# Where the high activations of the projections begin in SBUF: 64 instead of 192 modulo 256 bytes

## The reference

```python
# block 1
proj = rms_norm(x, norm1_w) @ w_in          # 2048 -> 5648 columns
attn = moba_attention(q, k, v)              # 8 heads of 128; one block of 256, so causal attention
y    = ssd_chunked_scan(xs, dt, a, bm, cm)  # 16 heads of 64, state 128
x = x + concatenate([attn, ssm]) @ w_out    # 2048 -> 2048
u = causal_dwconv(rms_norm(x, norm2_w) @ w_up, ...)       # 2048 -> 11264
x = x + (silu(u_gate) * u_val) @ w_down     # 5632 -> 2048
# block 2
mod = silu(c) @ w_ada + b_ada               # shift, scale, gate
proj = (rms_norm_2(x, g) * (1 + scale) + shift) @ w_in    # 2048 -> 7168 columns
y_a, y_r = dilated attention (8 heads), retention in both directions (4 heads)
out = rms_norm_2(x + gate * (concatenate([y_a * silu(z_a), y_r * silu(z_r)]) @ w_out), final_gain)
```

## Time and profile before

| | us |
|---|---|
| median of three runs | 1658.18 |
| the profiled execution, device time | 1657.61 |
| its span, first to last instruction | 1655.9 |
| TensorE busy with matmuls | 1608.4 |
| VectorE busy | 1159.8 |
| ScalarE busy | 807.2 |

### The profile page before, as it was taken

How to read it: one execution, slowest core, us unless ns; L and a number is a source line. 1 busy time by engine, 2 the same in 40 slices (tenths; PEclk the granted TensorE clock), 3 DMA queues, 4 the chain that set the end, 5 groups by cost and what they waited for, 6 DMA issues and landing times.

```text
span 1655.9 us, 33704 instructions
## 1 busy us (share of the span) xinstructions
PE 1608.4 (97%) x13254; PEld 1578.9 (95%) x13254; DVE 1159.8 (70%) x1357; ACT 807.2 (49%) x973; POOL 26.3 (2%) x53
## 2 busy tenths in 40 slices
PE   7999999989999999999999999999799999999997
PEld 7998899989999999999999999999799999999996
DVE  6676677765678888888888888676664544664755
ACT  6444355544554544545445454444454543445542
POOL 0000000000000000000000000000000000000000
PEclk9999999999999999999999999999999999999998
DMA  8453344455548777787777775555455555355451
GB/s 344 138 177 128 128 151 143 153 181 187 182 164 334 261 267 293 254 303 267 261 284 260 304 267 206 189 189 181 150 181 189 185 185 170 136 165 173 159 179 51
DMA packets 85187, 336.17 MB, mean 203 GB/s; under 512 B 9456, under 2 KB 9712, under 8 KB 78704
## 3 DMA queue, kind: packets, MB, share of 16 engines
q1 hardware_dynamic: 77328, 281.05, 49.0%
q0 software_dynamic: 7056, 51.38, 8.4%
q10 hardware_dynamic: 720, 2.52, 0.4%
HBM read 332.82 MB, written 2.10 MB: 202 GB/s over the span
## 4 chain that ended last, share of the span: by engine, by line
PE 72%; DVE 5%; issue 2%; ACT 1%; DVEq 0%; ACTq 0%
PE PS L1096 23%; PE PS L1098 23%; PE PS L1100 23%; DVE ada_w L931 1%; DVE wlo L586 1%; ACT whi L254 1%; PE PS L1197 1%; DVE UV L889 1%; PE PS L1164 1%; PE PS L1342 0%; DVE X L1083 0%; PE PS L1183 0%; DVE X L602 0%; DVE rb L620 0%; PE PS L1143 0%
## 5 line engine op out<-in xcount | busy, mean ns | idle before, releaser
L1096 PE MATMUL PS<-gh,whi 128*128 128x256 f32 x3520 | 999.4, 284 | 14.5 <-DVE wlo L586 9.4
L1098 PE MATMUL PS<-gl,whi 128*128 128x256 f32 x3520 | 985.1, 280 | 0.0
L1100 PE MATMUL PS<-gh,wlo 128*128 128x256 f32 x3520 | 983.9, 280 | 0.0
L586 DVE TENSOR_TENSOR wlo<-raw,whi 128x1024 fp32r<-128x1024 f32 x528 | 644.8, 1224 | 432.0 <-ACT whi L254 430.6
L254 ACT ACTIVATE whi<-raw 128x1024 fp32r<-128x1024 f32 x528 | 557.4, 1059 | 731.0 <-PE PS L1100 728.4
L1096 PEld LDWEIGHTS PS<-gh,whi 128*128 128x128 f32 x3520 | 664.5, 189 | 21.8 <-issue 20.5
L1098 PEld LDWEIGHTS PS<-gl,whi 128*128 128x128 f32 x3520 | 663.5, 188 | 2.8 <-issue 1.9
L1100 PEld LDWEIGHTS PS<-gh,wlo 128*128 128x128 f32 x3520 | 663.0, 188 | 0.0
L1096 PE MATMUL PS<-ah,whi 128*128 128x256 f32 x704 | 197.5, 281 | 10.5 <-DVE UV L889 6.8
L1098 PE MATMUL PS<-al,whi 128*128 128x256 f32 x704 | 196.1, 279 | 0.0
L1100 PE MATMUL PS<-ah,wlo 128*128 128x256 f32 x704 | 196.0, 278 | 0.0
(11 more groups left out here) (187 smaller groups left out, 804.3 us busy)
## 6 DMA issues: line engine op xcount, KB each, us to landing
raw<-weights SPq DMA_DIRECT2D x528, 512.0 KB, 3.4
ada_w<-w_ada POOLq DMA_DIRECT2D x48, 1024.0 KB, 5.1
outT<-X SPq DMA_DIRECT2D x4, 512.0 KB, 2.6
X<-xT SPq DMA_DIRECT2D x3, 512.0 KB, 8.8
c<-const ACTq DMA_DIRECT2D x1, 1536.0 KB, 6.7
c_act<-c_rows POOLq DMA_DIRECT2D x1, 1024.0 KB, 9.0
X<-xT SPq DMA_DIRECT2D x2, 256.0 KB, 4.9
prm<-params ACTq DMA_DIRECT2D x1, 276.5 KB, 4.2
```

The source lines that it names most:

```text
L586: dve.tensor_tensor(wlo[:, j % SPLIT, :], raw[:, j, :], whi[:, j % SPLIT, :].bitcast(F32), ALU.subtract).then_inc(s_lo, 1)
L1096: pe.matmul(out[:, t, :], whi[:, b, w], hi[:, kt, :], start=first and half == 0 and t % 2 == 0, stop=False, skip_group_check=True)
L1098: pe.matmul(out[:, t, :], whi[:, b, w], lo[:, kt, :], start=False, stop=False, skip_group_check=True)
L1100: mm = pe.matmul(out[:, t, :], wlo[:, b, w], hi[:, kt, :], start=False, stop=last and half == 1, skip_group_check=True)
```

## The change

A pad ahead of `gh` grows from 64 to 192 bytes, and one of 128 bytes is put between `gh` and `gl`. `gh` then begins at 64 modulo 256, `gl` at 192 as before. All that lies behind them (parameters, constants, the `ada_w` buffers, the areas of both blocks) is 256 bytes further up, at the same residue modulo 256. No instruction is added, removed or moved.

```diff
         wlo, _ = place("wlo", [P, SPLIT, 1024], F32R)
-        at[0] += 64
+        at[0] += 192
         gh, _ = place("gh", [P, DT, S], F32R)
+        at[0] += 128
         gl, _ = place("gl", [P, DT, S], F32R)
         at[0] += 64
         prm, _ = place("prm", [P, N_PARAMS])
```

## The result

The changed kernel is slower: a median of 1665.43 us against 1657.79, four runs each, ratio 1.0045 (95% interval 1.0032 to 1.0059). I had forecast 1641 us. The time lies inside the range that I gave, but on the other side of no change. The profiled execution, 1662.1 us with a span of 1660.4, is 4.5 us above that of before. Ratios compare fast executions alone, which leaves out one of `tail256` (3539 us) and one of `wlo0` (4333 us).

A forecast was written before the change was run, and what follows sets the result against it. TensorE's matmul pace was taken to bound the kernel. From 1657.6 us, 19.7 gained in the projections and 2.8 given back to waits made 1640.7, so 1641 us, range 1618 to 1673.

The forecast's parts named there:

- TensorE's pace is the time, and nothing else is touched: Whole kernel: TensorE is busy 1608.4 of 1655.9 us, so only a change of the matmuls' pace can move the time.
- Two paces, 113.3 and 117.8 ns, kept while residues stay alike: Distances between matmul starts: 2.720 or 2.827 us a unit, set by where weight load and moving read begin.
- The Trainium skill's rule that I weighed: SBUF reads: weight loads have their own read port, so the moving operand's residue is worth nothing and the sum is zero.
- A triple of the changed kernel takes 346 ns: Projections: three matmuls take 119 + 113.3 + 113.3 ns, 2.768 us a unit, for 19.7 us gained.
- part (1) of the sum: The 440 units on `gh`/`gl`: 22.5 us gained by 382 slow units, 2.8 us lost by 58 fast ones.
- rows 5: Trace at 617.38 us: a fast stretch on `ah`/`al` passes to `gh`/`gl`; one distance is 119 ns, then all 117.8.
- The second bound of that paragraph: Projections: the way back to 64 costs too, 351 ns a triple, a gain of 7.3 - 5.1 = 2.2 us.
- The 58 fast units: Units on `gh`/`gl` already at 113.3 ns: each loses 0.048 us, 2.8 us in all.
- The rival "nothing": Projections: the paces come from something else, or the triple averages 351 to 353 ns; 1658 us, chance 0.12.
- The slower rival: Every projection unit: switching costs both ways and never settles, 355 to 358 ns a triple, 1670 to 1680 us; chance 0.27.
- `ah`/`al` at nothing: The 88 units on `ah`/`al`: residues kept, effect taken as nothing, within 3.1 us gained and 6.3 lost.
- The wait given back in the loop: Feed-forward loop: TensorE waits longer for VectorE, 2.8 us given back over 8 passes; 8 us at the full 340 ns.

The follow-up runs named there:

- tail256: Against the kernel before: `gh` and `gl` kept at 192 modulo 256, everything behind them 256 bytes further up; 1657.59 us, ratio 0.9988.
- wlo0: Against the kernel before: `wlo` at 0 instead of 128 modulo 256, `gh` at 64, `gl` at 192; 1694.76 us, ratio 1.0225.
- both64: Against the kernel before: `gh` and `gl` both at 64 modulo 256 instead of 192, weights left at 128; median 1635.38 us, ratio 0.9870.
- all_moved: Against the kernel before: `whi` and `wlo` both at 0 modulo 256 instead of 128, `gh` and `gl` left at 192; 1639.73 us, ratio 0.9894.
- read_high: The changed kernel, but the projections' second product reads `gh` in place of `gl`, which is still written at 192; median 1641.73 us, 0.9918 of the kernel before.
- wlo0_act64: Against the kernel before: `wlo` at 0 modulo 256 instead of 128, `gh` and `gl` both at 64; 1620.18 us, ratio 0.9779.
- mirror: Against the kernel before: `whi` at 0 modulo 256 instead of 128, `wlo` at 128, `gh` and `gl` at 192; 1627.0 us, ratio 0.9825.
- fewer_steps: The changed kernel with the three products reordered for odd output tiles, so the moving residue changes twice in six matmuls, not four times; 1665.26 us.
- step32: Against the kernel before: `gh` at 64 and `gl` at 96 modulo 256 instead of both at 192; 1675.63 us, ratio 1.0116.
- both0: Against the kernel before: `gh` and `gl` both at 0 modulo 256 instead of 192, weights left at 128; 1674.64 us, ratio 1.0109.
- wlo0_act192: Against the kernel before: `wlo` at 0 modulo 256 instead of 128, `gh` and `gl` left at 192; 1657.07 us, ratio 0.9998.

## Why the prediction was wrong, point by point

- *TensorE's pace is the time, and nothing else is touched.* Right. Where the slow pace stays 353.3 ns, the span follows the count: 44 fewer fast units give +4.5 us (4.7 by the count), 130 more (`both64`) -10.5 us (13.9), 163 more (`all_moved`) -17.5 us (17.4), 251 more (`read_high`) -24.3 us (26.8), and in `wlo0_act64` 406 more -37.9 us (43.3).
- *Two paces, 113.3 and 117.8 ns, kept while residues stay alike, and set by where both reads begin.* Right that the residues set them: `read_high`, `all_moved` and `mirror` show it. "Kept" holds only between waits: before the change five stretches on `ah`/`al` were fast ahead of a wait and slow behind it, with the residues alike. The Trainium skill's rule that I weighed ("SBUF — State Buffer", section "A bandwidth-pool intuition that's wrong (but worth ruling out)": a second, independent read port for weight loads, and contention only from a port lock or a starved descriptor generator), by which the sum is zero, doesn't hold for this pair of reads: 1620 to 1695 us with nothing but pads moved.
- *A triple of the changed kernel takes 346 ns.* This is the step that failed, in part (1) of the sum. I took the price of one step from 64 to 192 from rows 5, where the step comes once between two stretches, and let the two other matmuls of the triple run at the fast pace. The changed kernel shows that triple, 346 ns, once at each passage; the next ones take 356 and 351, and the mean stays 353.3. `fewer_steps` shows why no price by the step could be right: half the steps, the same 353.3. The second bound of that paragraph, 351 ns with the way back, was nearer. It would have given 2.2 us less, still the wrong sign. The triple at which losses equal gains was wrong too: 352.7 ns is named, but by the same terms it is 351.6 (440 units at 2.813 us take as long as 382 at 2.827 and 58 at 2.720), so 353.3 lies clearly on the slower side.
- *The 58 fast units.* I priced their loss at 0.048 us each; it is 0.107, 6.2 us. The rival "nothing" named today's slow triple, 353.4 ns, and put 1658 us on it. That was an error in its own terms: with that triple the 58 fast units go, and 1657.6 + 6.2 = 1664 us. The rival with the right pace had the wrong time, and would have belonged to the slower side.
- *The slower rival.* Its mechanism, that a stretch with a step in each triple never settles, is what happened. Its price, 355 to 358 ns, wasn't paid by this kernel; `step32` paid it (356.7), and `wlo0` more (362.7).
- *`ah`/`al` at nothing.* 14 more were fast, 1.5 us gained in the profiled execution, inside my bounds of 3.1 and -6.3.
- *The wait given back in the loop.* TensorE's waits for `UV` went from 6.8 to 7.1 us; there was no gain to give back. In `wlo0_act64`, where there was, the feed-forward part (432 to 1201 us before, 422 to 1173 there) is 18.9 us shorter, 204 more fast units make 21.8: 2.9 us given back, where I charged 8 for that case.
- *Not explained.* The medians differ by 7.6 us and the profiled executions by 4.5. In the profiled execution 73 units on `ah`/`al` were fast; fewer in the timed ones would do it (each is 0.107 us), but only the profiled one can be counted. `fewer_steps`, at the same 353.3 ns, fits that: 41 are fast there, 32 fewer, and its span of 1663.8 us is 3.4 us longer, which is 32 x 0.107. And the runs don't say how the two reads meet inside the memory. Any picture of it has to give 340.0 for differences of 64, 64 and 192 when `wlo` makes the 192, and 353.3 when `gl` does.

## What to carry to other kernels

When matmuls stream back to back, look at the distance between their starts before their durations or the busy share: two paces of the same instruction, each kept for tens of microseconds, can mean that its operands' addresses matter, as they did here, and pads are then a cheap thing to try. Give the moving operands of one triple the same residue modulo 256 bytes; here every step between them cost the fast pace. Alike isn't enough (`both0`, `wlo0_act192`): the differences to the weights have to be tried as well. A price read from a passage between two stretches holds for that passage, and before it is multiplied by a whole loop, ask what state it leaves behind for the next instruction.

## What the runs showed of the hardware that I had not expected

- `whi` and `wlo` half a period of 256 bytes apart, activations alike and 64 below `whi`, leave the fast pace as the only one that lasts: 523 of 528 units at 113.3 ns in `wlo0_act64`, against 200 of 440 and 47 of 88 with the two weight tiles alike (`both64`).
- The same spacing with activations that step as well gives the slowest pace, 362.7 ns a triple (`wlo0`). The two steps aren't interchangeable.
- A step of 32 bytes between high and low activations costs more than one of 128: 356.7 against 353.3 ns a triple.
